# Scores and copy of head 0 in a differential-attention encoder: tile 1 in the second session, the copy further up

## The chip, the cores and the metric

The kernel runs on one core of one Trainium2 chip. The metric is the device time of one execution in microseconds (us), the median of several. All durations below are microseconds unless marked ns.

## The reference

Two layers over a sequence of 512 rows with 1024 features. Each layer has a mixer of three branches (a gated causal convolution with layer norm and silu, a differential attention, a spatial gate), a cross attention to 256 memory rows, and a convolutional feed-forward part. What matters here is the attention branch, and that the convolution's norm runs beside it:

```python
def one_block(args):                       # one of 4 blocks of 128 queries
    ...
    logits = jnp.einsum('bqhmd,bkhmd->bhmqk', q_blk, k).astype(f32) * scale + bias[None, :, None]
    logits = jnp.where(visible, logits, NEG_INF)
    p = jax.nn.softmax(logits, axis=-1)
    attn = p[:, :, 0] - lam * p[:, :, 1]   # two maps per head
    return jnp.einsum('bhqk,bkhe->bqhe', attn.astype(v.dtype), v)

merged = (gates[:, :, 0] * (ya @ w_br[0]) + gates[:, :, 1] * (yb @ w_br[1])
          + gates[:, :, 2] * (yc @ w_br[2]))
```

There are 4 heads with 2 maps (m = 0, 1) of 64 features each. A query block qb sees the keys up to its own block, so its score tile is 128 x 128(qb+1).

## The kernel before, in words

Every product of the model is done in three terms: each operand is split into a rounded head and a tail (the rest), and TensorE adds head x head, head x tail and tail x head. The weights come in units of 128 x 2048, numbered 0 to NU-1 in each layer (`plan`). A unit goes through four hands: SyncE loads it into `raw` (L571), ScalarE rounds it to `w_hd`, VectorE (or GpSimd) makes `w_tl` as the difference, and TensorE uses it (`product`, L1699, L1700 for the head terms, L1715 for the tail term). There are two buffers of each, so unit g+2 is loaded when the tail of unit g is made. Most products write two PSUM banks (a pair) and may start only when the pair's last product has been read (label `ev...`).

Each engine's program is one list, written out by hand in order of the units k: nothing is scheduled, and each engine does its list strictly in that order. All ScalarE work goes through the helper at L724. Engines wait for each other by counters: `line.done` marks an instruction with labels, `line.need`, `line.at` wait for them.

The attention is spread over the units 13 to 26 behind their products (`ATT`). Head h has these jobs:

- A (unit 13+3h) and B (unit 14+3h): TensorE makes the score tiles of both maps (`attention`). Map 0 uses rows 0 to 63 of the array and map 1 rows 64 to 127, so two neighbouring tiles of different maps run side by side. `TILES_OF` says which tiles, in pairs, `SC_AT` into which bank and column. For heads 0, 1 and 3 each tile is made of three terms, head 2 has one fp32 product. A takes query blocks 0, 1 and 2, B takes block 3. Tile (0, 1) and tile (1, 1) lie in bank 6 both, so the second waits for the first (`A_first`).
- VectorE reads each tile (`scores`, L1147), adds the bias and takes the row's maximum; ScalarE takes exponentials; VectorE combines the two maps (`combine`, L1159 to L1165) and turns the result in blocks of 32 x 32 (L1168). SyncE sends it to DRAM and back in four pieces (L546, L549, `turn`), and ScalarE copies them in order (label `att`, 128 x 1280).
- D (unit 16+3h): TensorE multiplies the probabilities with the values (L1808) into bank 7 (`misc`). It waits for that copy.

`IN_ORDER_AT` places the copies: head h's behind the two tanh of the gate in unit 16+3h. Beside head 0 runs the norm of the convolution: its sums are turned by TensorE in unit 15 (`conv_sums`, L1587, into bank 7), VectorE scales four tiles (L1437), ScalarE makes of each tile an affine form and its tanh (in unit 15, behind `CLN + 2`), and VectorE multiplies them (L1442). Behind these stand, in unit 16, VectorE's reads of the gate product (L1319), ScalarE's two tanh on them, and the copy of head 0.

Of the kernel before, what the change touches and what calls it, by code (L numbers as in the profile page):

```python
# [37 lines left out]
HEADS = 4  # L38
# [195 lines left out]
ATT0 = 13  # L234
# [4 lines left out]
for _h in range(HEADS):  # L239
    ATT.setdefault(ATT0 + 3 * _h + 3, []).insert(0, ("D", _h))  # L240
    if _h >= MOVED:
# [6 lines left out]

SO = [0, 128, 384, 768]
SC_AT = {(0, 0): (4, 384), (0, 1): (6, 0), (0, 2): (4, 0), (0, 3): (4, 0),  # L250
         (1, 0): (5, 384), (1, 1): (6, 256), (1, 2): (5, 0), (1, 3): (5, 0)}

TILES_OF = {"A": ((0, 1), (1, 2), (0, 2), (1, 0), (0, 0), (1, 1)), "B": ((0, 3), (1, 3))}
QK_HEADS = {11: (0, 1), 20: (3,)}
QK_TAILS = {21: 3}
QK_AT = {0: (4, 6), 1: (5, 7), 3: (2, 3)}
YA_ROUNDED = CLN + 5
IN_ORDER_AT = {ATT0 + 3 * _h + 3: _h for _h in range(HEADS)}
TURN_AT = {ATT0 + 3 * _h + 6: _h for _h in range(HEADS)}
OUT_AT = {ATT0 + 3 * _h + 8: _h for _h in range(MOVED)}  # L260

# [101 lines left out]
def build(nc, x_t, mem_t, units, pvec, bs, lam, w_st, rel_bias, onehot, ident_in, out, counts):  # L363
    ctx = ExitStack()
    with ctx:
# [26 lines left out]
        moved = s_sb[:, 0, :].rearrange("p (a t j) -> p t a j", a=4, j=32)  # L392
# [321 lines left out]
        def _(act):  # L714
# [100 lines left out]
            def cross_heads(h):  # L815
                op(y_hd[:, h, :], ps[:, X_OUT[h], :], labels=(f"yx_head{h}",), needs=(f"xpv{h}",))

            def heads_of_outputs(k):
                for h in YB_SPLIT.get(k, ()):
                    if h == 2:  # L820
                        act.wait_ge(tensor_done, line.at("B3"))
                    if h < MOVED:
                        act.wait_ge(o_in, 64 * (l * MOVED + h + 1))
                        op(in_order(y_hd[:, h, :]), turned_rows(q_sb[:, h, :]), ACT.Identity, (f"yb_head{h}",),
                           scale=col(l, "sub_g"))
                    else:
                        op(y_hd[:, h, :], q_sb[:, h, :], labels=(f"yb_head{h}",), needs=(f"ot{h}",))

            for l in range(DEPTH):
                line.begin(l)  # L830
                for k in range(NU):
                    for e, kind, arg in () if last_units(l, k) else UNIT_KINDS[k]:
# [14 lines left out]
                        elif kind == "u":  # L847
                            view = u_sb[:, 2 * arg:2 * arg + 2, :]
                            op(view, view, ACT.Gelu_apprx_tanh, (f"gelu_u{arg}",), (f"ev{e}",))
                        elif kind in ("w", "v"):  # L850
                            dst, f = (vn, ACT.Gelu_apprx_tanh) if kind == "w" else (v_sb, ACT.Copy)
                            for t in range(TB if arg else 0):
                                op(dst[:, t, :], ps[:, WIDE_BANK[kind] + t, :], f, (f"ev{e - 1 + t // 2}",),
                                   ("n0_rs", f"{kind}_tokens{t}"), scale=rs0[:, t:t + 1])
                            if arg:
                                next_head(k)
                        elif kind == "sv":
                            if arg == 0:
                                squares("c", lambda t: cg[:, C_OUT[t], PAD:], range(KB), lambda t: (f"c_cent{t}",))
                            for g in (2 * arg, 2 * arg + 1):  # L860
                                op(y_hd[:, g, :], tmp[:, g, :], labels=(f"yc_head{g}",), needs=(f"yc_src{g}",))
                        elif kind in ("gg", "g2"):
                            pos, j = arg
                            if kind == "g2":
                                j -= 1
                            if k == LAST_TURN:
                                heads_of_outputs(k)
                            for i in range(2):
                                view = tmp[:, gate_at(pos, j) + i, :]
                                op(view, view, ACT.Tanh, (f"th_g{pos}_{j + i}",), (f"raw_g{pos}_{j + i}",),  # L870
                                   scale=0.5, bias=col(l, "gate_b", BRANCH_OF[pos] * KD + j + i))
                            if k in IN_ORDER_AT:
                                h = IN_ORDER_AT[k]
                                act.wait_ge(att_in, 64 * (l * HEADS + h + 1))
                                op(att_t.rearrange("p t (a j) -> p t a j", a=4), moved, labels=(f"att{h}",))
                        elif kind == "xk":
                            op(kx_hd[:, 2 * arg:2 * arg + 2, :], ps[:, b:b + 2, 0:MEM], labels=(f"kx_head{arg}",))
                        elif kind == "xq" and arg == 0:
                            next_head(k)
                            query_heads(0, e)  # L880
                        elif kind == "up":
                            f0 = 4 * (arg % 2)
                            if arg == FIRST_UPS - 1:
                                next_head(k)
                            for i in range(2):
                                c = arg + NF * i
                                op(ft[:, f0 + i, :], tmp[:, 2 * (arg % 2) + i, :], ACT.Identity, (f"lin{arg}_{i}",),
                                   (f"up_src{arg}_{i}",) + ((f"act_tail{arg - 2}",) if arg >= 2 else ()),
                                   scale=col(l, "ffn_w", 3 * c + 2), bias=col(l, "ffn_b", c))
                            next_head(k + 1 if arg == FIRST_UPS - 1 else k)  # L890
                            op(ft[:, f0 + 2, :], ft[:, f0, :], ACT.Tanh, (f"th_f{arg}",), (f"conv_f{arg}_0",), scale=0.5)
                            op(ring_hd[:, arg % 8, :], ft[:, f0 + 2, :], labels=(f"act_head{arg}",),
                               needs=(f"act_src{arg}",), scale=0.5)
# [18 lines left out]
                    if k == CLN + 2:  # L912
                        for i in range(KB):
# [2 lines left out]
                               (f"c_norm{i}", "cs") + ((f"ya_src{i - 2}",) if i >= 2 else ()),  # L916
                               scale=col(l, "cln_g", i), bias=col(l, "cln_b", i))
                            op(th, z, ACT.Tanh, (f"th_c{i}",), (), scale=0.5)
                    for h in QK_HEADS.get(k, ()):
                        if h == 3:  # L920
                            act.wait_ge(tensor_done, line.at(f"e{ENTRY_OF['bb', (0, 6)]}"))
# [83 lines left out]
        def _(dve):  # L1005
# [132 lines left out]
            def scores(job, h):  # L1138
# [3 lines left out]
                for n, (m, qb) in enumerate(TILES_OF[job]):  # L1142
# [6 lines left out]
                        in1=bias_t[:, h % 2, S - w:S], scale=1.0, scalar=-3.0e38, op0=ALU.add, op1=ALU.max,  # L1149
                        accum_out=mx[:, 4 * m + qb:4 * m + qb + 1]), f"sc_free{job}_{h}", needs=(f"{job}{h}",) + free,  # L1150
                       plain=True, independent=min(n, 1))
                part = slice(0, 3) if job == "A" else slice(3, 4)
                op(lambda: dve.tensor_scalar(mneg.rearrange("p (m q) -> p m q", q=4)[:, :, part],
                                             mx.rearrange("p (m q) -> p m q", q=4)[:, :, part], -1.0, None, ALU.mult),
                   f"neg{job}_{h}")
# [414 lines left out]
        def _(pe):  # L1570
# [206 lines left out]
            def attention(job, h):  # L1777
                if job in "AB":
# [10 lines left out]
                        parts = ((q_sb[:, h], k_sb[:, h]),)  # L1789
                    for n in range(0, len(TILES_OF[job]), 2):  # L1790
                        pair = TILES_OF[job][n:n + 2]
                        if (1, 1) in pair:
                            pe.wait_ge(tensor_done, line.at(f"A_first{h}"))
                        for p, (q, key) in enumerate(parts):
                            for m, qb in pair:
                                bank, c0 = SC_AT[m, qb]
                                rows = slice(64 * m, 64 * m + 64)
                                i = pe.matmul(ps[:, bank, c0:c0 + P * (qb + 1)], q[rows, P * qb:P * qb + P],  # L1798
                                              key[rows, 0:P * (qb + 1)], start=p == 0, stop=p == len(parts) - 1)
                                if (m, qb) == (0, 1) and p == len(parts) - 1:  # L1800
                                    line.done(i, f"A_first{h}")
                    line.done(i, f"{job}{h}")
                elif job == "D":
                    pe.wait_ge(scalar_done, line.at(f"att{h}"))
# [63 lines left out]
                spread("n0", 4, rs0)  # L1868

            def conv_sums():  # L1870
                turned_sums("c", "c_cent3")

            for l in range(DEPTH):
                line.begin(l)
# [249 lines left out]
```

## Time and profile before

| | us |
|---|---|
| median of 3 runs | 1760.96 (1760.45 to 1761.63) |
| the profiled execution | 1761.88 |
| its span | 1760.1 |
| TensorE busy | 1741.1 (99%) |
| VectorE busy | 1287.1 (73%) |
| ScalarE busy | 745.7 (42%) |
| GpSimd busy | 491.3 (28%) |
| mean granted TensorE clock | 0.995 |

The profile is one execution; its times count from the span's start. An engine is busy while it works on an instruction; a matmul's end is modelled, so the start of the next one is the surer mark. In square brackets behind a row stands the idle time ahead of it and what ended it. PEld is TensorE's loading of weights, which lies beside the matmuls.

### The profile page before, as it was taken

How to read it: one execution, taken by the hardware profiler on the slowest of the kernel's cores; microseconds unless marked ns; L12 is line 12 of the kernel's file. 1: busy time of each engine (PE TensorE's matmuls, PEld its weight loads, DVE VectorE, ACT ScalarE, POOL GpSimd, SP SyncE). 2: the span in 40 equal slices, each digit the busy share in tenths (PEclk: the TensorE clock that was granted, in tenths of full speed). 3: DMA queues.
4: the chain of work that ended last, by engine and by line, in shares of the span. 5: the costliest groups of instructions: out<-in, count | busy, mean ns of one | idle time of the engine just before them, and what ended most of it. 6: DMA issues, size and time to landing. Idle time of an engine off the chain costs nothing. (4 is left out here: it accounts for less than half of the span.)

```text
span 1760.1 us, 21739 instructions
## 1 busy us (share of the span) xinstructions
PE 1741.1 (99%) x8127; PEld 1447.8 (82%) x8127; DVE 1287.1 (73%) x1696; ACT 745.7 (42%) x951; POOL 491.3 (28%) x204
## 2 busy tenths in 40 slices
PE   9999899999999999999999998999999999999998
PEld 7888788888888888888888887888888888888888
DVE  7998768664678776577779786775746797685585
ACT  4234555443564443343432345553445544343343
POOL 4453000103034244444133620010030332444440
PEclk9999999999999999999999999999999999999999
DMA  6532244422322332232232323444222223322321
GB/s 216 191 120 72 102 165 137 172 96 96 120 75 94 120 109 85 98 117 82 110 144 72 144 72 120 168 140 148 96 96 96 96 96 120 118 74 96 120 74 71
DMA packets 40777, 199.60 MB, mean 113 GB/s; under 512 B 4828, under 2 KB 14300, under 8 KB 20320
## 3 DMA queue, kind: packets, MB, share of 16 engines
q1 hardware_dynamic: 38460, 186.35, 30.0%
q0 software_dynamic: 1648, 11.54, 1.7%
q8 instruction: 64, 1.05, 0.2%
q10 hardware_dynamic: 564, 0.33, 0.1%
q14 instruction: 41, 0.34, 0.1%
HBM read 186.06 MB, written 14.49 MB: 114 GB/s over the span
## 5 line engine op out<-in xcount | busy, mean ns | idle before, releaser
L1699 PE MATMUL ps<-x_hd,w_hd 128*128 128x512 f32 x1568 | 612.3, 390 | 0.1
L1700 PE MATMUL ps<-x_tl,w_hd 128*128 128x512 f32 x1568 | 610.4, 389 | 0.0
L606 POOL TENSOR_TENSOR w_tl<-raw,w_hd 128x2048 fp32r<-128x2048 f32 x79 | 366.0, 4632 | 534.5 <-ACT w_hd L724 392.6
L724 ACT ACTIVATE w_hd<-raw 128x2048 fp32r<-128x2048 f32 (+2 forms) x159 | 298.1, 1875 | 321.7 <-PE ps L1700 231.9
L1715 PE MATMUL ps<-x_hd,w_tl 128*128 128x512 f32 x1568 | 373.4, 389 | 0.0
L1699 PEld LDWEIGHTS ps<-x_hd,w_hd 128*128 128x128 f32 x1568 | 294.3, 188 | 62.6 <-issue 0.7
L1715 PEld LDWEIGHTS ps<-x_hd,w_tl 128*128 128x128 f32 x1568 | 294.1, 188 | 61.0
L1700 PEld LDWEIGHTS ps<-x_tl,w_hd 128*128 128x128 f32 x1568 | 294.4, 188 | 60.5
L1699 PE MATMUL ps<-ring_hd,w_hd 128*128 128x512 f32 (+1 forms) x640 | 241.1, 381 | 0.0
L1700 PE MATMUL ps<-ring_tl,w_hd 128*128 128x512 f32 (+1 forms) x640 | 239.8, 379 | 0.0
L1402 DVE SCALAR_TENSOR_TENSOR merged<-merged 128x512 f32<-128x512 f32 x44 | 183.4, 4167 | 20.7 <-ACT merged L724 20.2
L1019 DVE TENSOR_TENSOR w_tl<-raw,w_hd 128x2048 fp32r<-128x2048 f32 x71 | 163.4, 2302 | 38.7 <-ACT w_hd L724 27.5
L1265 DVE TENSOR_TENSOR resid<-resid,ps 128x512 f32<-128x512 f32 x120 | 77.1, 684 | 115.0 <-PE ps L1715 111.8
L1181 DVE SCALAR_TENSOR_TENSOR ps<-cg,pv_all,ps 128x512 f32<-128x512 f32 x232 | 154.5, 747 | 0.0
L1715 PE MATMUL ps<-ring_hd,w_tl 128*128 128x512 f32 (+1 forms) x640 | 151.5, 379 | 0.0
L1699 PEld LDWEIGHTS ps<-ring_hd,w_hd 128*128 128x128 f32 x640 | 120.4, 188 | 26.7 <-issue 3.0
L1700 PEld LDWEIGHTS ps<-ring_tl,w_hd 128*128 128x128 f32 x640 | 120.4, 188 | 22.2
L1715 PEld LDWEIGHTS ps<-ring_hd,w_tl 128*128 128x128 f32 x640 | 115.9, 188 | 22.4
L724 ACT ACTIVATE ring_hd<-merged 128x512 fp32r<-128x512 f32 x44 | 27.8, 633 | 225.2 <-DVE merged L1404 225.2
L724 ACT ACTIVATE merged<-tmp,pv_all 128x512 f32<-128x512 f32 x88 | 71.9, 817 | 117.3 <-DVE tmp L1382 113.2
L1393 DVE SCALAR_TENSOR_TENSOR merged<-tmp,pv_all,merged 128x510 f32<-128x510 f32 (+1 forms) x176 | 120.2, 744 | 0.9 <-ACT merged L724 0.9
L1382 DVE TENSOR_TENSOR tmp<-ps,sq 128x512 f32<-128x512 f32 x88 | 56.7, 686 | 82.4 <-PE ps L1715 81.7
(229 smaller groups left out, 1654.0 us busy)
## 6 DMA issues: line engine op xcount, KB each, us to landing
raw<-units SPq DMA_DIRECT2D x154, 1024.0 KB, 4.8
att_dram<-s_sb SPq DMA_DIRECT2D x8, 640.0 KB, 2.9
s_sb<-att_dram SPq DMA_DIRECT2D x32, 160.0 KB, 3.4
bias_t<-bias_tiles POOLq DMA_DIRECT2D x8, 256.0 KB, 5.5
cg<-mem_t POOLq DMA_DIRECT2D x2, 1024.0 KB, 7.2
resid<-x_t POOLq DMA_DIRECT2D x1, 2048.0 KB, 8.1
resid_dram<-resid POOLq DMA_DIRECT2D x1, 2048.0 KB, 7.4
resid<-resid_dram POOLq DMA_DIRECT2D x1, 2048.0 KB, 8.2
```

Source lines behind the costliest of these rows:

```text
L606: line.done(pool.tensor_tensor(w_tl[:, k % 2, :], raw[:, k % 2, :], w_hd[:, k % 2, :].bitcast(F32), ALU.subtract), of_unit("tail", g))
L724: line.done(act.activation(out, in_, func, **kw), *labels)
L1019: op(lambda: dve.tensor_tensor(w_tl[:, slot, :], raw[:, slot, :], w_hd[:, slot, :].bitcast(F32), ALU.subtract), of_unit("tail", g), needs= ...
L1181: op(lambda: dve.scalar_tensor_tensor(dst, src, w, acc, ALU.mult, ALU.add), independent=1)
L1265: op(lambda: dve.tensor_tensor(dst, dst, ps[:, banks(e) + i, :], ALU.add), f"{tag}_{j + i}", f"ev{e}", needs=(f"e{e}",), independent=i)
L1382: op(lambda: dve.tensor_tensor(src, ps[:, b + i, :], r_all, ALU.mult), f"up_src{arg}_{i}", f"ev{e}", needs=(f"e{e}",), independent=i)
L1393: op(lambda: dve.scalar_tensor_tensor(dst[:, sh:S], src[:, 0:S - sh], col(l, "ffn_w", 3 * c + 2 - sh), dst[:, sh:S], ALU.mult, ALU.add), f ...
L1402: op(lambda: dve.scalar_tensor_tensor(th, th, 1.0, ft[:, f0, :], ALU.add, ALU.mult), needs=(f"th_f{arg}",))
L1699: pe.matmul(dst, w_hd[:, slot, w], hd[:, src, :], start=kc == 0, stop=False)
L1700: i = pe.matmul(dst, w_hd[:, slot, w], tl[:, src, :], start=False, stop=False)
L1715: i = pe.matmul(dst, w_tl[:, slot, w], hd[:, src, :], start=False, stop=kc == nk - 1)
```

## The change

Two things are moved, for both layers. Tile (0, 1) and tile (1, 1) of every head go from A to B; (0, 1) stays in bank 6 and (1, 1) goes to bank 7, the bank of the sums and of D. With that the wait `A_first` goes, A and B have equal tiles in every pair, the slices of the negated maxima follow, and the conv sums wait for the last reading of B0 as well. And the copy of head 0 goes from unit 16 to unit 15, behind the affine form and the tanh of the second conv tile; the copies of heads 1 to 3 stay.

```diff
 SC_AT = {(0, 0): (4, 384), (0, 1): (6, 0), (0, 2): (4, 0), (0, 3): (4, 0),
-         (1, 0): (5, 384), (1, 1): (6, 256), (1, 2): (5, 0), (1, 3): (5, 0)}
-TILES_OF = {"A": ((0, 1), (1, 2), (0, 2), (1, 0), (0, 0), (1, 1)), "B": ((0, 3), (1, 3))}
+         (1, 0): (5, 384), (1, 1): (7, 0), (1, 2): (5, 0), (1, 3): (5, 0)}
+TILES_OF = {"A": ((0, 2), (1, 2), (0, 0), (1, 0)), "B": ((0, 3), (1, 3), (0, 1), (1, 1))}
...
-IN_ORDER_AT = {ATT0 + 3 * _h + 3: _h for _h in range(HEADS)}
+IN_ORDER_AT = {ATT0 + 3 * _h + 3: _h for _h in range(1, HEADS)}
...
+            def probabilities_in_order(h):
+                act.wait_ge(att_in, 64 * (l * HEADS + h + 1))
+                op(att_t.rearrange("p t (a j) -> p t a j", a=4), moved, labels=(f"att{h}",))
...
                             op(th, z, ACT.Tanh, (f"th_c{i}",), (), scale=0.5)
+                            if i == 1:
+                                probabilities_in_order(0)
...
-                part = slice(0, 3) if job == "A" else slice(3, 4)
+                part = slice(0, 4, 2) if job == "A" else slice(1, 4, 2)
...
-                        if (1, 1) in pair:
-                            pe.wait_ge(tensor_done, line.at(f"A_first{h}"))
...
-                                if (m, qb) == (0, 1) and p == len(parts) - 1:
-                                    line.done(i, f"A_first{h}")
...
-                turned_sums("c", "c_cent3")
+                turned_sums("c", "c_cent3", "sc_freeB_0")
```

**ScalarE, units 14 to 16 of layer 0.** `sq<-cg` and `cg<-sq` are a conv tile's affine form and tanh, `tmp<-tmp` the tanh of unit 16's gate, 128x1280 the copy of head 0, `w_hd<-raw` the heads of units 17 and 18. Before:

```order
L724 ACTIVATE w_hd<-raw 128x2048 [waits scalar_done,weights_in1,tensor_done]
L724 ACTIVATE sq<-cg,pv_all 128x512 [waits scalar_done,tensor_done,vector_done]
L724 ACTIVATE cg<-sq 128x512 [waits scalar_done]
L724 ACTIVATE sq<-cg,pv_all 128x512 [waits scalar_done,tensor_done,vector_done]
L724 ACTIVATE cg<-sq 128x512 [waits scalar_done]
L724 ACTIVATE sq<-cg,pv_all 128x512 [waits scalar_done,tensor_done,vector_done]
L724 ACTIVATE cg<-sq 128x512 [waits scalar_done]
L724 ACTIVATE sq<-cg,pv_all 128x512 [waits scalar_done,tensor_done,vector_done]
L724 ACTIVATE cg<-sq 128x512 [waits scalar_done]
L724 ACTIVATE tmp<-tmp,pv_all 128x512 [waits scalar_done,vector_done] x2
L724 ACTIVATE s_sb<-s_sb 128x1280 [waits scalar_done,att_in]
L724 ACTIVATE w_hd<-raw 128x2048 [waits scalar_done,weights_in0,tensor_done]
```

Now:

```order
L724 ACTIVATE w_hd<-raw 128x2048 [waits scalar_done,weights_in1,tensor_done]
L724 ACTIVATE sq<-cg,pv_all 128x512 [waits scalar_done,tensor_done,vector_done]
L724 ACTIVATE cg<-sq 128x512 [waits scalar_done]
L724 ACTIVATE sq<-cg,pv_all 128x512 [waits scalar_done,tensor_done,vector_done]
L724 ACTIVATE cg<-sq 128x512 [waits scalar_done]
L724 ACTIVATE s_sb<-s_sb 128x1280 [waits scalar_done,att_in]
L724 ACTIVATE sq<-cg,pv_all 128x512 [waits scalar_done,tensor_done,vector_done]
L724 ACTIVATE cg<-sq 128x512 [waits scalar_done]
L724 ACTIVATE sq<-cg,pv_all 128x512 [waits scalar_done,tensor_done,vector_done]
L724 ACTIVATE cg<-sq 128x512 [waits scalar_done]
L724 ACTIVATE tmp<-tmp,pv_all 128x512 [waits scalar_done,vector_done] x2
L724 ACTIVATE w_hd<-raw 128x2048 [waits scalar_done,weights_in0,tensor_done]
```

The copy has moved ahead of the third and fourth conv tile and of the gate's tanh; these and the head of unit 18 stand behind it and its wait for `att_in`.

**TensorE, the scores of head 0 in layer 0** (`ring_hd`, `ring_tl` are the split queries and keys; lines behind 816 stand 4 further down in the kernel after). The second and third pair of A, before:

```order
L1798 MATMUL ps<-ring_hd 128x384
L1798 MATMUL ps<-ring_hd 128x128
L1798 MATMUL ps<-ring_tl,ring_hd 128x384
L1798 MATMUL ps<-ring_tl,ring_hd 128x128
L1798 MATMUL ps<-ring_hd,ring_tl 128x384
L1798 MATMUL ps<-ring_hd,ring_tl 128x128
L1798 MATMUL ps<-ring_hd 128x128 [waits tensor_done]
L1798 MATMUL ps<-ring_hd 128x256
L1798 MATMUL ps<-ring_tl,ring_hd 128x128
L1798 MATMUL ps<-ring_tl,ring_hd 128x256
L1798 MATMUL ps<-ring_hd,ring_tl 128x128
L1798 MATMUL ps<-ring_hd,ring_tl 128x256
```

A now, and the first instruction of unit 14:

```order
L1800 MATMUL ps<-ring_hd 128x384 [waits vector_done]
L1800 MATMUL ps<-ring_hd 128x384
L1800 MATMUL ps<-ring_tl,ring_hd 128x384 x2
L1800 MATMUL ps<-ring_hd,ring_tl 128x384 x2
L1800 MATMUL ps<-ring_hd 128x128 x2
L1800 MATMUL ps<-ring_tl,ring_hd 128x128 x2
L1800 MATMUL ps<-ring_hd,ring_tl 128x128 x2
L1703 MATMUL ps<-x_hd,w_hd 128x512 [waits vector_done,scalar_done]
```

B of head 0 now, whose first four rows were all of it before:

```order
L1800 MATMUL ps<-ring_hd 128x512 [waits vector_done]
L1800 MATMUL ps<-ring_hd 128x512
L1800 MATMUL ps<-ring_tl,ring_hd 128x512 x2
L1800 MATMUL ps<-ring_hd,ring_tl 128x512 x2
L1800 MATMUL ps<-ring_hd 128x256 x2
L1800 MATMUL ps<-ring_tl,ring_hd 128x256 x2
L1800 MATMUL ps<-ring_hd,ring_tl 128x256 x2
```

The 256-wide tiles are gone from A, with the wait inside it, and stand at the end of B.

## Rows read from the trace of the kernel before

**Rows 1.** Waits of TensorE: engine line <- what released it: us, times, longest.
```profile
PE ps L1808 <- ACT s_sb L724: 11.1, 2, 5.7
```

**Rows 2.** Order of time, TensorE, units 16 and 17: start us, us, engine line operation.
```profile
200.06 1.98 PE L1715 MATMUL ps<-ring_hd,w_tl 128*128 128x512 f32 x8
...
207.78 4.64 PE L1808 MATMUL ps<-v_sb,s_sb 128*128 128x128 f32 x20 [5.75 <-ACT s_sb L724]
...
214.36 0.50 PE L1699 MATMUL ps<-x_hd,w_hd 128*128 128x512 f32 x1
...
1077.93 4.63 PE L1808 MATMUL ps<-v_sb,s_sb 128*128 128x128 f32 x20 [5.33 <-ACT s_sb L724]
...
1084.64 0.50 PE L1699 MATMUL ps<-x_hd,w_hd 128*128 128x512 f32 x1
```

**Rows 3.** Windows, layer 0: us; PE, PEld, DVE, ACT, POOL busy (x); granted clock.
```profile
206.00:208.00 2.00, 0.22 (x1) 0.22 (x2) 0.96 (x2) 1.79 (x3) 0.00 (x0) 0.72 0.00 0
...
210.00:212.00 2.00, 2.00 (x12) 2.00 (x10) 0.00 (x0) 0.00 (x0) 0.00 (x0) 0.50 0.00 0
```

**Rows 4.** Order of time, TensorE: head 2 D, head 3 A, product; head 3 B, product.
```profile
286.24 2.39 PE L1808 MATMUL ps<-v_sb,s_sb 128*128 128x128 f32 x20
...
288.56 0.44 PE L1798 MATMUL ps<-ring_hd 64*128 64x256 f32 x2
...
289.97 0.50 PE L1699 MATMUL ps<-x_hd,w_hd 128*128 128x512 f32 x1
...
301.07 0.50 PE L1798 MATMUL ps<-ring_hd 64*128 64x512 f32 x2
...
301.97 0.50 PE L1699 MATMUL ps<-ring_hd,w_hd 128*128 128x512 f32 x1
```

**Rows 5.** Order of time, ScalarE, units 14 to 16 of layer 0.
```profile
184.85 0.72 ACT L724 ACTIVATE s_sb<-s_sb,mneg 128x512 f32<-128x512 f32 x1 [0.74 <-DVE mneg L1153]
...
199.46 0.63 ACT L724 ACTIVATE cg<-sq 128x512 f32<-128x512 f32 x1
...
206.46 1.27 ACT L724 ACTIVATE s_sb<-s_sb 128x1280 f32<-128x1280 f32 x1
```

**Rows 6.** The four pieces (L549) of head 0: issues, first and last start, landing; both layers.
```profile
L549 SPq DMA_DIRECT2D s_sb<-att_dram x4: 340/432/433, 195.3 to 196.6; - x4
...
DMA to landing us min/median/max: 2.8/3.3/3.7
...
L549 SPq DMA_DIRECT2D s_sb<-att_dram x4: 326/432/434, 1065.5 to 1066.8; - x4
...
DMA to landing us min/median/max: 2.8/3.5/4.6
```

**Rows 7.** Order of time, VectorE, units 13 to 16 of layer 0.
```profile
172.46 0.42 DVE L1147 CUSTOM_DVE_ANT_0 s_sb<-ps,bias_t 128x256 f32<-128x256 f32 x1 [0.29 <-DVE tmp L1338]
...
172.81 0.08 DVE L1147 DVE_READ_ACCUMULATOR2_ANT mx<- 128x1 f32 x1
...
183.30 0.69 DVE L1147 CUSTOM_DVE_ANT_0 s_sb<-ps,bias_t 128x512 f32<-128x512 f32 x1 [0.17 <-issue]
...
184.64 0.17 DVE L1153 TENSOR_SCALAR mneg<-mx 128x2 f32<-128x2 f32 x1
...
188.35 0.20 DVE L1159 RECIPROCAL rc<-sm 128x8 f32<-128x8 f32 x1
...
204.11 1.29 DVE L1319 TENSOR_TENSOR tmp<-ps,r 128x512 f32<-128x512 f32 x2
...
212.46 1.13 DVE L1194 TENSOR_SCALAR tmp<-ps,rc 128x128 f32<-128x128 f32 x4 [5.37 <-PE ps L1808]
```

**Rows 8.** Order of time, units 13 and 15: VectorE's bank read, then TensorE.
```profile
165.30 1.62 DVE L1333 SCALAR_TENSOR_TENSOR tmp<-ps,pv_all,wsbs 128x512 f32<-128x512 f32 x2
...
167.06 0.47 PE L1699 MATMUL ps<-x_hd,w_hd 128*128 128x512 f32 x1
...
182.78 0.60 PE L1587 MATMUL ps<-ident,ssum 128*128 128x128 f32 x4
```

More of the change, by code:

```diff
@@ L872, in _ @@
                             if k in IN_ORDER_AT:
-                                h = IN_ORDER_AT[k]
-                                act.wait_ge(att_in, 64 * (l * HEADS + h + 1))
-                                op(att_t.rearrange("p t (a j) -> p t a j", a=4), moved, labels=(f"att{h}",))
+                                probabilities_in_order(IN_ORDER_AT[k])
                         elif kind == "xk":
```

## The prediction

> **What bounds the kernel now.** I read the table of the page first: TensorE is busy 99% of 1760.1 us, so only time in which it stands still, runs at the low clock or streams more columns than it must can be won. The view of waits, for TensorE, has one entry over 2 us: twice, 11.1 us in all, it waits for ScalarE before the matmuls of L1808 [rows 1]. These are the value products of head 0 (job D, unit 16), once in each layer. The order of time shows the place [rows 2]: unit 16's last product starts at 200.06 and lasts 1.98, and D0 starts at 207.78, after 5.75 idle; in layer 1 the idle is 5.33 before 1077.93.
>
> The wait costs more than itself. The windows [rows 3] show the granted clock at a mean 0.72 in 206 to 208 and 0.50 in 210 to 212: TensorE went from 2.4 to 1.2 GHz while it stood idle, near 206.9. So D0 and the scores of head 1 behind it (A1) take 6.58 (207.78 to 214.36) and 6.71 (1077.93 to 1084.64) [rows 2], where D of head 2 and A of head 3 take 3.73 at full clock (286.24 to 289.97) [rows 4].
>
> What D0 waits for is the copy that puts the turned probabilities in order (206.46 to 207.73) [rows 5]. ScalarE does it behind the two tanh of unit 16's gate, and these behind the whole conv chain. Its data were there long before: the four pieces were issued at 195.3 to 196.6 and took at most 3.7 to land, so by 200.3; in layer 1, 1066.8 plus at most 4.6, so by 1071.4 [rows 6].
>
> **Part 1: the copy moves up.** It now stands behind the second tanh of the conv chain, which ends at 200.09 [rows 5], in layer 1 at 1070.24 (that layer runs the same pattern 870.15 later: 1077.93 against 207.78). So it starts at about 200.3 and 1071.4 (the landing decides), takes 1.27, and is done at 201.6 and 1072.7, before TensorE comes to D0. The wait is gone. What is queued behind the copy on ScalarE now comes later: the third and fourth conv tiles. In layer 0 they slip 1.4 (copy and step), in layer 1, where ScalarE also stands 1.1 for the last piece, 2.5. VectorE's last conv step and then its two gate reads (204.11 on, 1.29 for both) [rows 7] slip by as much: the second read ends at 206.9 instead of 205.4, and at 1078.0 instead of 1075.55. TensorE needs that read: it frees the banks of unit 17's product, which stands behind A1.
>
> **Part 2: tile 1 in the second session.** In a session both maps run side by side on 64 rows each. The session A of before streams 768 columns per map and term (128, 256, 384) and B 512; now A has 512 and B 768. The two swap. From [rows 4]: A took 1.41 (288.56 to 289.97) and B 0.90 (301.07 to 301.97). So A should cost 0.9 to 1.05 now (two of its tiles are only 128 wide; I take 1.0) and B 1.22 (0.90 plus 3 times 256 columns at 2.4 GHz, 0.32) to 1.41. Over a head that is -0.2 to +0.15: nothing. But A0's part is not won at all: the product behind it starts at 167.06, and VectorE's read of its banks ends at 166.92 [rows 8], so TensorE waits there instead.
>
> VectorE drops two 256-wide score steps in A and adds them in B, 0.35 each (172.46 to 172.81) [rows 7]. It works without a pause here, so B0's scoring starts 0.7 to 1.0 earlier, at about 182.4, and ends after about 1.25 (183.30 to 184.64, less the step to the negation) plus 0.70, at about 184.3. In layer 1 it is the same within 0.2. ScalarE's exponentials of B0 start at 184.85 now [rows 5], so at about 184.5; four of at most 0.9 each (0.72 and the read of the sum behind it) end by 188.1, and VectorE takes up the sums at 188.35 [rows 7]. So the turned probabilities leave at their old time.
>
> **Part 3: the added wait.** Bank 7 now holds scores of B0, so the conv sums in unit 15 also wait for B0's scoring. They start at 182.78 now [rows 8], and would stand at 183.1 after the longer B0. They get in at about 184.3, so TensorE idles 1.1 to 1.2 in each layer. I bound this by 0 (VectorE comes earlier) and 1.9 (nothing of A's saving reaches B0). All behind it is 1.45 later: unit 16 ends near 203.5 (202.05 plus 1.45) and near 1074.05.
>
> **The sum**, at the start of unit 17's product. Layer 0: TensorE is at D0 at 203.5, D0 takes 2.32 (286.24 to 288.56) [rows 4], A1 1.0, so 206.8; the gate read ends at 206.9; start at 206.95 against 214.36, -7.4. Layer 1: 1074.05 plus 2.32 plus 1.0 is 1077.4, but the read ends at 1078.0; start at 1078.1 against 1084.64, -6.5. Of each about 4 is idle, 2.8 the clock; 0.1 to 0.75 goes back to the new wait for the gate read. In the rest of a layer B1, A2, B2, A3 and B3 add and save in turn: +0.3, -0.4, +0.4, -0.4, +0.3, so +0.2, and +0.5 for both layers. -7.4 - 6.5 + 0.5 is -13.4.
>
> Does it stay? Behind unit 17, VectorE stood idle 5.37 before it could read D0 (212.46) [rows 7]; this reserve is used up, but by my count of its list (gate merge to 208.4, reading of D0, scoring of A1, tail weights) it is done with unit 18's tails near 213.6, and TensorE needs them near 223, behind unit 17's 48 products, B1 and unit 18's head terms. Nothing later waits for a fixed time: loads follow the tails, the tails follow TensorE. I cost the later units at zero for that reason; without this cover each us VectorE is late is one us per layer.
>
> The profiled execution took 1761.9, of which 1760.1 are the span; so 1748.5 for it. The median of the runs is 0.9 lower: **1747.6 us**.
>
> **Rivals.**
>
> *The wait moves further (14%).* The gate read, or the last piece, comes later than I read it, and unit 17's product stands still. For it: in layer 1 one piece already took 4.6, and VectorE, ScalarE and TensorE meet here within 0.1 to 0.7. Against it: in layer 0 no piece took over 3.7. Each us is paid once per layer; 2 us in each give 1751.6.
>
> *The clock falls once more (4%).* If the idle of 1.1 at unit 15, or one at unit 17, brings the low level as now, about 2.8 comes back per layer, what D0 and A1 lose to it now (6.58 against 3.73) [rows 2, 4]: 1753.2. Against it: at full idleness the clock held from 202.0 to 206.9.
>
> *Slower: the clock stays low through units 15 to 17 (3%).* The new wait is followed by short blocks (four transposes, the spread, D0), and if TensorE stayed at 1.2 GHz from 184.3 to 206.9, 22.5 us of work would take twice as long: +22.5 and -6.7 per layer, 1792.6. It decides from the point where the low stretch holds more than 6.7 us of full-speed work. Against it: the only low stretch of now costs 2.8 in all, although D0 and A1 in it are short blocks. The Trainium skill (TensorE: Matmul & The Clock Gate, "A second HAM failure mode: psum-queue depth-cycling") describes such a kernel: short idles between groups of matmuls make the clock swing between its two levels. By that rule this change, which puts three short idles where one long one was, would be the 1792.6; this trace does not show it, since its one fall follows the one long idle.
>
> *It does not do what it says (2%).* If the pieces landed 5 us later than their rows, D0 would wait as before and the time stay at about 1760.
>
> **Numbers.** My forecast has 77%. Measured against no change, about 0.2% (3.5 us) can be told apart. Faster by more: forecast and the first two rivals, 0.95. Within: 0.02. Slower: 0.03. The low end of the range has the added wait at 0, no wait for the gate read and A and B at their low values (-2.3, -0.9, -1.3): 1743.1. The high end takes in the first two rivals: 1753.5.
>
> **What would show it.** In the profile of the changed kernel: no wait of L1808's group for ScalarE; a granted clock of 1.00 from 200 to 216; the copy between the second and third conv tile; about 1.1 idle before the conv sums, ended by VectorE's scoring; the value products of head 0 at 2.3 instead of 4.6; unit 17's product at 207.0 and, with layer 0's gain, near 1071. Wrong would be a new pause in front of unit 17 of over 2 us, a low clock in units 15 to 17, or a gain at unit 17 that is gone by unit 22.

## The result, and the profile after

The changed kernel takes 1748.12 us, the median of 6 runs (1747.71 to 1749.45); the kernel before takes 1761.05 (6 runs, 1759.82 to 1761.63). The ratio is 0.9929, 95% interval 0.9916 to 0.9941. 12.9 us are gone; 13.4 were predicted. The profiled execution took 1749.45 with a span of 1747.6, and its mean granted clock is 0.999 where it was 0.995.

The view of waits, for TensorE, lists what is left (the line numbers stand 4 higher than before):

```profile
PE ps L1591 <- DVE mx L1151: 2.2, 2, 1.3
...
PE ps L1703 <- ACT tmp L724: 1.1, 1, 1.1
PE ps L1703 <- DVE tmp L1337: 0.9, 2, 0.5
```

The value products (L1808) are not in it any more: of their 11.1 us [rows 1] nothing is left. In their place stand the conv sums (L1591), which wait for VectorE's scoring of B0, and once the product of unit 17 (L1703). The third line is 0.45 in each layer before the product behind A0 (167.75 in layer 0), where the prediction had said that TensorE would wait for VectorE's read instead of winning A's shorter time. TensorE in order of time, layer 0 and then layer 1: conv sums, last product of unit 16, D0, A1, product of unit 17:

```profile
185.28 0.66 PE L1591 MATMUL ps<-ident,ssum 128*128 128x128 f32 x4 [1.30 <-DVE mx L1151]
...
202.57 1.98 PE L1719 MATMUL ps<-ring_hd,w_tl 128*128 128x512 f32 x8
204.39 2.39 PE L1808 MATMUL ps<-v_sb,s_sb 128*128 128x128 f32 x20
206.71 0.44 PE L1800 MATMUL ps<-ring_hd 64*128 64x384 f32 x2
...
207.83 0.47 PE L1703 MATMUL ps<-x_hd,w_hd 128*128 128x512 f32 x1
...
1048.42 0.66 PE L1591 MATMUL ps<-ident,ssum 128*128 128x128 f32 x4 [0.92 <-DVE mx L1151]
...
1067.53 2.39 PE L1808 MATMUL ps<-v_sb,s_sb 128*128 128x128 f32 x20
1069.85 0.44 PE L1800 MATMUL ps<-ring_hd 64*128 64x384 f32 x2
...
1071.99 0.47 PE L1703 MATMUL ps<-x_hd,w_hd 128*128 128x512 f32 x1 [1.07 <-ACT tmp L724]
```

These rows answer to [rows 2]: D0 takes 2.32 (204.39 to 206.71) and A1 1.12, where the two took 6.58. In the windows the granted clock stays at 1.00, so 2.4 GHz, where [rows 3] had 0.72 and 0.50; the last three windows are 8 us long and begin at the conv sums of each layer and at unit 17 of layer 1:

```profile
206.00:208.00 2.00, 1.95 (x21) 1.72 (x20) 1.70 (x4) 0.79 (x2) 0.00 (x0) 1.00 0.00 0
208.00:210.00 2.00, 2.00 (x10) 1.61 (x10) 1.76 (x4) 1.89 (x2) 0.00 (x0) 1.00 0.00 0
...
184.00:192.00 8.00, 6.72 (x32) 5.66 (x33) 7.47 (x17) 3.44 (x10) 1.02 (x1) 1.00 0.57 227
1048.00:1056.00 8.00, 7.58 (x36) 6.36 (x37) 7.47 (x15) 4.27 (x9) 1.02 (x1) 1.00 0.47 181
1071.00:1079.00 8.00, 7.01 (x31) 5.83 (x32) 7.11 (x18) 6.88 (x17) 0.00 (x0) 1.00 0.00 0
```

ScalarE in order of time, the copy in both layers, and VectorE's two reads of unit 16's gate product behind it:

```profile
201.09 1.27 ACT L724 ACTIVATE s_sb<-s_sb 128x1280 f32<-128x1280 f32 x1 [0.40 <-DMA s_sb<-att_dram]
...
1065.27 1.27 ACT L724 ACTIVATE s_sb<-s_sb 128x1280 f32<-128x1280 f32 x1 [1.42 <-DMA s_sb<-att_dram]
```

```profile
206.39 1.29 DVE L1323 TENSOR_TENSOR tmp<-ps,r 128x512 f32<-128x512 f32 x2
...
1070.55 1.29 DVE L1323 TENSOR_TENSOR tmp<-ps,r 128x512 f32<-128x512 f32 x2
```

The copy now waits for its data (0.40 and 1.42), where before the data waited for the copy. In layer 1 the second gate read ends at 1071.84 and unit 17's product starts at 1071.99. The bracket there names ScalarE's tanh, but the start lies 0.15 behind the end of the read; in the first experiment below, where the bracket names VectorE, it lies 0.14 behind (1070.38 plus 1.29, against 1071.81). It is the read that TensorE waits for. The same holds in layer 0: the read ends at 207.68 and unit 17's product starts at 207.83, 0.15 behind. No bracket stands there, because the modelled ends of A1's matmuls cover it; but where the read is early (the copy behind the third tile, below) A1 takes 1.00 from start to start, not 1.12, so about 0.12 of it is this wait.

**Where the time came from.** The two profiled executions, part by part, at the starts of TensorE's rows (the marks 161.40, 1031.94 and 1196.28 of before are 162.09, 1025.60 and 1183.88 now):

| stretch | before | after | difference |
|---|---|---|---|
| start to the first mark, ahead of the change | 161.40 | 162.09 | +0.69 |
| to unit 17 of layer 0 | 52.96 | 45.74 | -7.22 |
| to the mark in layer 1 | 817.58 | 817.77 | +0.19 |
| to unit 17 of layer 1 | 52.70 | 46.39 | -6.31 |
| to the mark behind the attention | 111.64 | 111.89 | +0.25 |
| to the end | 563.82 | 563.72 | -0.10 |
| sum | 1760.1 | 1747.6 | -12.50 |

The first line is no effect of the change: the first 162 us are the same program, and the profiled executions of the kernels below lie between 161.28 and 162.03 there. Nothing was given back later.

The rows also say what the two gains are made of. Layer 0: the idle before D0 was 5.75 and 1.30 of new idle stands before the conv sums, so 4.45; D0 and A1 take 3.44 instead of 6.58, so 3.14, of which 0.29 is A1's (1.12 instead of 1.41) and the rest the clock; B0 costs 0.36 more. That is 7.23. Layer 1: 5.33 less 0.92 and 1.07 is 3.34; D0 and A1 without the idle behind them take 3.39 instead of 6.71, so 3.32; less 0.36 that is 6.30.

The scores of head 3 answer to [rows 4]. The starts of A3, the product behind it, B3 and the product behind that:

```profile
282.31 0.44 PE L1800 MATMUL ps<-ring_hd 64*128 64x384 f32 x2
...
283.30 0.50 PE L1703 MATMUL ps<-x_hd,w_hd 128*128 128x512 f32 x1
...
294.41 0.50 PE L1800 MATMUL ps<-ring_hd 64*128 64x512 f32 x2
...
295.67 0.50 PE L1703 MATMUL ps<-ring_hd,w_hd 128*128 128x512 f32 x1
```

A takes 0.99 instead of 1.41, B 1.26 instead of 0.90.

### The profile page after: what moved, and what is told of

It is laid out like the page before. It is cut to its first block and busy times, and to the rows that moved or that the text cites. A ratio compares the mean times of both kernels' runs of the same rounds, so it can differ in the third digit from the quotient of the medians.

```text
span 1747.6 us, 21739 instructions
## 1 busy us (share of the span) xinstructions
PE 1735.7 (99%) x8127; PEld 1442.4 (83%) x8127; DVE 1286.9 (74%) x1696; ACT 745.7 (43%) x951; POOL 490.7 (28%) x204
## 5 line engine op out<-in xcount | busy, mean ns | idle before, releaser
L1703 PE MATMUL ps<-x_hd,w_hd 128*128 128x512 f32 x1568 | 612.2, 390 | 2.0 <-ACT tmp L724 1.1
L1703 PEld LDWEIGHTS ps<-x_hd,w_hd 128*128 128x128 f32 x1568 | 294.3, 188 | 64.2 <-issue 2.8
L1703 PE MATMUL ps<-ring_hd,w_hd 128*128 128x512 f32 (+1 forms) x640 | 241.2, 381 | 0.0
L1703 PEld LDWEIGHTS ps<-ring_hd,w_hd 128*128 128x128 f32 x640 | 120.3, 188 | 24.5 <-issue 0.7
```

The source lines that it names most:

```text
L1703: pe.matmul(dst, w_hd[:, slot, w], hd[:, src, :], start=kc == 0, stop=False)
```

## Experiments

My theory: the whole gain is the copy's (idle and clock), and the tiles bring nothing. The rivals: the tiles carry a part of it; the new wait at the conv sums costs its full length; the clock falls in other places too. Diffs are against the changed kernel except where said.

### The copy alone

Bank, tiles and `A_first` are those of the kernel before; against that kernel:

```diff
-IN_ORDER_AT = {ATT0 + 3 * _h + 3: _h for _h in range(HEADS)}
+IN_ORDER_AT = {ATT0 + 3 * _h + 3: _h for _h in range(1, HEADS)}
...
                             op(th, z, ACT.Tanh, (f"th_c{i}",), (), scale=0.5)
+                            if i == 1:
+                                probabilities_in_order(0)
```

> Only the copy of head 0 is moved; the tiles stay as before. Theory (the whole gain is the copy): D0 starts when TensorE comes to it, 1.45 us earlier than in the change since the added wait is absent; but unit 17's product is held by VectorE's gate read (206.9 and 1078.0 on before's times), so it starts where the change's does; 13.4 to 14.4 us below before, 1746.6 to 1747.6. Rival (the moved tiles bring part of the gain): at least 2 us above the change, 1750 or more.

Measured: 1748.93 (4 runs, 1747.75 to 1749.76), ratio to before 0.9931 (0.9915 to 0.9948). The changed kernel's ratio is 0.9929, so the two can't be told apart. The forecast of 1746.6 to 1747.6 was 1.3 too low at its near end, and the rival's 1750 or more did not come either. From the marks of the table to unit 17 this kernel takes 46.15 and 46.17, the changed one 45.74 and 46.39: the same sum within 0.2. In its view of waits the conv sums are missing, and the wait before unit 17 is longer:

```profile
PE ps L1703 <- DVE tmp L1323: 3.0, 2, 1.5
```

In order of time it stands in both layers:

```profile
208.18 0.47 PE L1703 MATMUL ps<-x_hd,w_hd 128*128 128x512 f32 x1 [1.49 <-DVE tmp L1323]
...
1071.81 0.47 PE L1703 MATMUL ps<-x_hd,w_hd 128*128 128x512 f32 x1 [1.49 <-DVE tmp L1323]
```

So TensorE gets to unit 17 earlier and waits there for the gate read. In the changed kernel 2.2 us stand before the conv sums and 1.1 before unit 17: the tiles move most of this wait further up, and the time stays.

### The tiles alone

```diff
-IN_ORDER_AT = {ATT0 + 3 * _h + 3: _h for _h in range(1, HEADS)}
+IN_ORDER_AT = {ATT0 + 3 * _h + 3: _h for _h in range(HEADS)}
...
-                            if i == 1:
-                                probabilities_in_order(0)
```

> Only the tiles are moved; the copy stays where it was. Theory: D0 still waits for the copy, which VectorE and ScalarE reach at the same time as before, so D0 starts at 207.8 again, after 4.3 us of idle instead of 5.75, because the added wait stands ahead of it; +0.5 us for the rest, 1761.5, if the clock falls as before. If 4.3 us of idle no longer bring the low clock, D0 and A1 give back 2.8 us per layer and it is 1755.5. Rival (the tiles bring part of the gain by themselves): 1757 to 1759 with the clock falling as before.

Measured: 1760.14 (10 runs, 1757.63 to 1761.44), ratio 0.9994 (0.9984 to 1.0003): no difference that can be told from noise, where 1761.5 was forecast, and not the rival's 1757 to 1759. The idle before D0 is 1.9 and 1.5 shorter than before [rows 2], since the later conv sums take it up (4.3 instead of 5.75 was forecast, it is 3.85). The clock falls all the same. In layer 0 the low stretch is shorter, from 207.8 to 211.2, and in layer 1 as long as before, 6.8 us, although the two idles are alike; the ten executions have mean clocks of 0.995 to 0.998, so this differs between executions too. D0 in both layers, the windows of layer 0, and one of 8 us in layer 1:

```profile
207.62 4.13 PE L1806 MATMUL ps<-v_sb,s_sb 128*128 128x128 f32 x20 [3.85 <-ACT s_sb L724]
...
1076.45 4.64 PE L1806 MATMUL ps<-v_sb,s_sb 128*128 128x128 f32 x20 [3.84 <-ACT s_sb L724]
```

```profile
206.00:208.00 2.00, 0.38 (x2) 0.39 (x3) 0.79 (x2) 1.79 (x3) 0.00 (x0) 0.94 0.00 0
208.00:210.00 2.00, 2.00 (x11) 2.00 (x11) 0.00 (x0) 1.59 (x1) 0.00 (x0) 0.50 0.00 0
210.00:212.00 2.00, 2.00 (x15) 1.88 (x15) 0.22 (x1) 0.00 (x0) 0.00 (x0) 0.70 0.00 0
...
1074.00:1082.00 8.00, 5.55 (x30) 5.33 (x30) 2.31 (x7) 4.12 (x4) 0.00 (x0) 0.57 0.00 0
```

### The copy later: behind the third and the fourth tanh

```diff
-                            if i == 1:
+                            if i == 2:
```

> The change, with the copy behind the third conv tile's tanh instead of the second's. Theory: in layer 1 ScalarE no longer stands for the last piece (1.4 us in the change), the gate read comes 1.1 us earlier and TensorE's wait before unit 17 (1.07 us) goes; in layer 0 nothing moves: 1 us below the change. Rival (that wait is not the gate read's): same as the change within 0.3 us, with the wait still there.

Measured: 1748.09 (4 runs, 1747.85 to 1748.3), ratio 0.9927 (0.9913 to 0.9942), so no different from the change, where 1 us less was forecast. The trace does show the forecast: in layer 1 the copy finds its data landed, the wait before unit 17 is gone, and from the mark to unit 17 that layer takes 45.26 instead of 46.39. The changed kernel's profiled execution was the slowest of its six (1749.45, median 1748.12); perhaps the others had less of this wait, but no trace of them exists.

```profile
1065.43 1.27 ACT L724 ACTIVATE s_sb<-s_sb 128x1280 f32<-128x1280 f32 x1
```

With `i == 3`, behind the last tanh:

> The change, with the copy behind the fourth conv tile's tanh. Theory: ScalarE reaches the copy at 204.0 (layer 0) and 1067.1 (layer 1) on the change's times and ends it 0.9 to 1.0 us after TensorE stands at D0; the gate read is 1.4 and 2.8 us earlier, so nothing waits before unit 17. Layer 0 +0.9, layer 1 -0.2: 0.7 us above the change, with a wait of L1808 for ScalarE of 1.0 us in each layer. Rival (the place of the copy within the conv chain does not matter): the change's time and no wait of D0.

Measured: 1749.91 (4 runs, 1749.5 to 1750.62), ratio 0.9936 (0.9921 to 0.9952). Now D0 waits for the copy again, 0.77 in each layer where 1.0 was forecast, and nothing waits before unit 17. To unit 17 the two layers take 0.94 more and 0.09 less than in the changed kernel, as forecast (+0.9 and -0.2); the medians lie 1.8 apart, and the four runs (from 1749.5) all lie above the six of the change (up to 1749.45).

```profile
204.52 2.50 PE L1808 MATMUL ps<-v_sb,s_sb 128*128 128x128 f32 x20 [0.77 <-ACT s_sb L724]
...
1068.60 2.50 PE L1808 MATMUL ps<-v_sb,s_sb 128*128 128x128 f32 x20 [0.77 <-ACT s_sb L724]
```

The three places lie within 1.8 us of each other and all over 11 us below before. What matters most is that the copy leaves the place behind the gate's tanh; among the places ahead of it, the place decides only which waits of 1.5 or less are left.

### The conv sums wait longer, for the tail of unit 16

```diff
             def conv_sums():
+                pe.wait_ge(vector_done, line.at(of_unit("tail", l * NU + 16)))
                 turned_sums("c", "c_cent3", "sc_freeB_0")
```

> The change, with the conv sums waiting also for the tail weights of unit 16, which VectorE makes behind B0's scoring; TensorE then idles 3.7 us there instead of 1.3 (layer 0) and 3.4 instead of 0.9 (layer 1). Theory: each us is paid once, less the wait before unit 17 in layer 1 that it hides: +2.4 and +1.3, 3.7 us above the change, and the clock stays at 2.4 GHz. Rival (an idle of this length brings the low clock too): a granted clock of 0.5 somewhere in units 15 to 17 and 2 to 6 us more on top.

Measured: 1756.54 (9 runs, 1755.73 to 1757.66), ratio 0.9976 (0.9966 to 0.9985): 8.4 above the change. The theory that only the added idle counts fell, and its rival held. TensorE in order of time, both layers, and the windows of layer 0:

```profile
187.57 0.66 PE L1591 MATMUL ps<-ident,ssum 128*128 128x128 f32 x4 [3.91 <-DVE w_tl L1023]
...
1054.84 0.66 PE L1591 MATMUL ps<-ident,ssum 128*128 128x128 f32 x4 [3.55 <-DVE w_tl L1023]
```

```profile
186.00:188.00 2.00, 0.43 (x5) 0.43 (x5) 1.51 (x1) 1.79 (x5) 0.00 (x0) 1.00 0.00 0
188.00:190.00 2.00, 2.00 (x10) 1.58 (x8) 1.53 (x5) 0.23 (x2) 0.76 (x1) 0.72 0.72 184
190.00:192.00 2.00, 2.00 (x6) 1.58 (x5) 1.97 (x5) 0.00 (x0) 0.26 (x1) 0.50 0.83 348
```

The clock falls only when TensorE is already working again, at about 188.9, and is back at about 192.3. The added idles are 2.6 in each layer, of which layer 1 hides 1.1 in its old wait before unit 17, so 4.2; two low stretches of 3.4 at half speed cost 3.4. That is 7.6, and trace against trace the way from the mark to unit 17 is 4.15 and 3.13 longer, 7.3. The traces leave nothing over; the medians lie 8.4 apart because the changed kernel's profiled execution was its slowest.

### Bank 7 read first

VectorE reads the tiles (0, 1) and (1, 1) of every B first, and the conv sums wait for these two alone (label `sc_seven_0` on head 0's read of bank 7, the second of them).

```diff
-                for n, (m, qb) in enumerate(TILES_OF[job]):
+                tiles = TILES_OF[job] if job == "A" else TILES_OF[job][2:] + TILES_OF[job][:2]
+                for n, (m, qb) in enumerate(tiles):
...
-                turned_sums("c", "c_cent3", "sc_freeB_0")
+                turned_sums("c", "c_cent3", "sc_seven_0")
```

> The change, but VectorE reads B0's tile in bank 7 ahead of the 512-wide tiles and the conv sums wait for that tile alone; nothing else moves. Theory: the wait of 1.3 and 0.9 us before the conv sums goes, TensorE comes to unit 17 that much earlier and waits there for the gate read, which stays where it is: the change's time within 0.4 us, with 1.2 and 2.0 us of idle before unit 17. Rival (the added wait costs its length): 2.2 us below the change.

Measured: 1749.32 (4 runs, 1749.03 to 1751.17), ratio 0.9932 (0.9914 to 0.995). The wait at the conv sums is gone and the time is no better: it has moved before unit 17, and in layer 1 to D0 as well, which waits 0.30 for the copy. TensorE in order of time, and the windows behind the second of these rows:

```profile
207.56 0.47 PE L1705 MATMUL ps<-x_hd,w_hd 128*128 128x512 f32 x1 [1.06 <-DVE tmp L1325]
...
1072.09 0.47 PE L1705 MATMUL ps<-x_hd,w_hd 128*128 128x512 f32 x1 [1.90 <-ACT tmp L724]
```

```profile
1072.00:1074.00 2.00, 1.91 (x6) 1.62 (x7) 1.63 (x3) 1.79 (x3) 0.00 (x0) 0.72 0.00 0
1074.00:1076.00 2.00, 2.00 (x6) 1.52 (x6) 1.72 (x7) 1.74 (x5) 0.00 (x0) 0.50 0.00 0
```

I had not expected the second of these rows to bring this: after 1.90 idle, with D0's 0.30 shortly before it, the clock went to 1.2 GHz. From 1072.86 to 1076.24 TensorE starts 8 matmuls, 0.42 apart; 0.23 apart they would take 1.8 instead of 3.4, so 1.6 is lost. The forecast (the change's time within 0.4) missed by that much in this execution. The profiled run took 1751.17, the three others 1749.03 to 1749.55, which fits a fall in the one and none in the others, at a mean clock of 0.998 against 0.999. Even these three lie 0.9 to 1.4 above the changed kernel's median.

### Idles of 2.4 and 3.3

To see from which idle on the clock falls, the conv sums wait for the first exponential of B0 on ScalarE, and in a second kernel for the second one (`expB_0_1_3`).

```diff
+                                op(view, view, ACT.Exp, (f"exp{job}_{h}", f"exp{job}_{h}_{m}_{qb}"), (f"neg{job}_{h}",),
...
             def conv_sums():
+                pe.wait_ge(scalar_done, line.at("expB_0_0_3"))
```

> The changed kernel, but the conv sums in unit 15 also wait for the first exponential of B0 on ScalarE. By the rows of the changed kernel that ends at 186.1 to 186.2 and TensorE starts at about 186.4 instead of 185.28: the idle grows from 1.30 to 2.4, in layer 1 from 0.92 to 2.0. Layer 1 stood 1.07 before unit 17 anyway, so it hides its share. Theory that only the idles of 3.5 and more bring the low clock: granted clock 1.00 from 184 to 194, time +1.1 for layer 0 and 0 to 0.2 for layer 1, so about 1749.3. Rival, that an idle of about 2 does it too, as the profiled run of the kernel with bank 7 read first hints (1.90 idle, then 0.50): the clock is 0.5 in 188 to 192, and each fall costs about 2.1 more (what the longer wait cost over its idles), so 1751.4 with one fall, 1753.5 with two.

> As the one before, but the wait is for the second exponential made (query block 3 of map 1), about 0.9 later: idle 3.3 in layer 0 and 2.9 in layer 1. Theory that only idles of 3.5 and more bring the low clock: clock 1.00 throughout, time +2.0 and +0.9, so about 1751.1. Rival, that it falls here too: +4.2 more, 1755.3, with windows of 0.50 in both layers.

The first: 1751.34 (4 runs), ratio 0.9944 (0.9927 to 0.996). Its profiled run took 1749.91 and shows the idles as meant and no fall. The two rows, and the window of 8 us about each:

```profile
185.83 0.66 PE L1591 MATMUL ps<-ident,ssum 128*128 128x128 f32 x4 [2.35 <-ACT s_sb L724]
...
1049.94 0.66 PE L1591 MATMUL ps<-ident,ssum 128*128 128x128 f32 x4 [1.98 <-ACT s_sb L724]
```

```profile
184.00:192.00 8.00, 6.17 (x29) 5.18 (x30) 7.48 (x17) 2.83 (x8) 1.02 (x1) 1.00 0.53 199
1048.00:1056.00 8.00, 6.06 (x29) 5.09 (x30) 7.47 (x17) 2.84 (x8) 1.02 (x1) 1.00 0.57 208
```

The three others took 1751.31 to 1751.47 at a mean clock of 0.998 against 0.999. So the profiled execution is near the theory's 1749.3 and the three others at the rival's 1751.4 with one fall: the same kernel holds the clock in one execution and, as far as mean clock and time tell, loses it once in the others. In which layer, no trace shows.

The second: 1755.09 (5 runs, 1754.39 to 1755.27), ratio 0.9964 (0.9951 to 0.9977), mean clock 0.997 in all five. The profiled one shows both outcomes, a fall after 3.25 in layer 0, and none after 2.89 in layer 1:

```profile
186.70 1.12 PE L1591 MATMUL ps<-ident,ssum 128*128 128x128 f32 x4 [3.25 <-ACT s_sb L724]
...
1054.44 0.66 PE L1591 MATMUL ps<-ident,ssum 128*128 128x128 f32 x4 [2.89 <-ACT s_sb L724]
```

```profile
184.00:186.00 2.00, 0.00 (x0) 0.00 (x0) 1.83 (x6) 0.98 (x3) 0.00 (x0) 0.90 0.63 266
186.00:188.00 2.00, 1.30 (x5) 1.25 (x6) 1.47 (x2) 1.81 (x6) 0.00 (x0) 0.50 0.00 0
...
190.00:192.00 2.00, 2.00 (x6) 1.52 (x6) 1.97 (x4) 0.00 (x0) 0.00 (x0) 0.50 0.75 307
...
1052.00:1060.00 8.00, 5.56 (x27) 4.65 (x28) 7.47 (x15) 2.83 (x8) 1.02 (x1) 1.00 0.46 185
```

By the medians it costs 7.0 over the change, near the rival's 1755.3; but of the rival's two falls the profiled execution has one, in a stretch twice as long. Trace against trace the way from the mark to unit 17 is 4.55 longer in layer 0 and 0.87 in layer 1, 5.4. The idles explain 2.9 (3.25 less 1.30 in layer 0; 2.89 less 0.92 in layer 1, of which 1.07 is hidden in the old wait before unit 17), the low stretch, in which TensorE works from 186.70 to about 192.4, another 2.8: 5.7, so nothing is left over in the traces. The rest of the 7.0 lies between executions: the changed kernel's profiled one was its slowest, this kernel's its fastest.

### All three waits taken away

VectorE makes the weight tail of unit 17 (2.3 us) ahead of the conv tiles, and later stands idle for ScalarE's tanh. Here the tail comes behind the second conv step (`ya_src1`), in that pause, and all four tiles, the tanh and the gate read come earlier. The copy stands behind the fourth tanh, where its data have landed or nearly so:

```diff
-                            if i == 1:
+                            if i == 3:
...
-                    if k in TAIL_MID:
+                    if k in TAIL_MID and k != CLN + 2:
...
+                            if i == 1:
+                                tail_of_unit(l * NU + k + 2)
```

> The copy behind the fourth conv tile as in the run before, and VectorE makes unit 17's tail weights behind the second conv tile's last step instead of ahead of the norm, so the conv chain runs 2.4 us earlier. Theory: the copy ends at 203.0, ahead of TensorE (204.4), the gate read near 205; no wait at D0 and none before unit 17; layer 0 the same as the change, layer 1 1.1 us earlier: 1.1 us below the change. Rival (tail weights made later hold unit 17 or the loads behind them): slower than the change, with a wait of L1715's products for VectorE.

Measured: 1748.0 (4 runs, 1747.85 to 1748.22), ratio 0.9925 (0.991 to 0.9941). No wait is left at D0 or unit 17, only the one at the conv sums. As with the copy behind the third tile, the forecast 1.1 shows in the trace (45.66 and 45.28 to unit 17, against 45.74 and 46.39) and not in the medians. With bank 7 read first added to it:

> The norm first, the copy behind the fourth conv tile, and VectorE reading bank 7's tile first. Theory: now that neither the gate read nor the copy holds TensorE, the 1.3 and 0.9 us before the conv sums are won as well: 1.1 + 2.1 = 3.2 us below the change, 1744.9. Rival (the added wait never cost anything): same as the run without the changed order.

Measured: **1745.51** (4 runs, 1745.44 to 1745.73), ratio 0.9911 (0.9896 to 0.9927). All of its waits of TensorE of 0.5 us or more:

```profile
PE ps L1611 <- POOL ones L627: 1.1, 1, 1.1
PE ps L1707 <- DVE tmp L1339: 0.9, 2, 0.5
PE ps L1956 <- POOL rs L623: 0.5, 1, 0.5
```

The forecast was 3.2 below the change, 2.6 came. Neither of the two edits alone gained anything that the runs can tell apart (1748.0 and 1749.32 against 1748.12). Together they bring 2.6, and 2.5 over the first of them alone, whose conv sums still wait 2.2. That 2.2 is worth something only once the gate read behind it is no longer late. Whether bank 7 read first on top of the copy behind the third tile would do as much was not run; there the gate read ends only 0.37 and 0.34 before unit 17's product starts, so it should run into it again.

## Why the prediction was right, and where it was off

The forecast was 1747.6 in a range of 1743.1 to 1753.5; 1748.12 came out, by the mechanism it named. Point by point:

- **The wait at D0 goes, and the clock stays up.** Right. The copy alone gives the whole gain, the tiles alone none that can be told from noise; -7.22 and -6.31 up to unit 17 stand against -7.4 and -6.5, and idle and clock share it as forecast (about 4 and 2.8 in layer 0; 3.3 and about 3 in layer 1).
- **The copy's time.** The landing decides, as forecast. In layer 1 the last piece took 4.9, where 4.6 was the largest [rows 6]; the copy waited 1.42, where I had 1.1. With bank 7 read first the last piece took 5.2 there.
- **The added wait.** Forecast 1.1 to 1.2 in each layer, measured 1.30 and 0.92. B0's scoring came 0.77 earlier against its surroundings (183.22, less the 0.69 of the start, against 183.30 [rows 7]), at the near end of my 0.7 to 1.0. The exponentials and the turned probabilities left at their old time, as forecast: the pieces were issued from 195.9 on, less 0.69 that is 195.2, against 195.3 [rows 6].
- **The gate read before unit 17.** The sum had 0.15 in layer 0 and 0.7 in layer 1; measured 0.12 (inside the 1.12 from A1's start to unit 17's) and 1.07. In layer 1 TensorE came earlier (its conv sums waited only 0.92) and the piece later.
- **A and B.** Forecast 1.0 and 1.22, measured 0.99 and 1.26. Over the rest of both layers +0.5 was forecast and +0.34 came (0.19, 0.25 and -0.10).
- **VectorE's reserve.** It is done with unit 18's tails at 215.0 (212.75 plus 2.29), less the start's 0.69 at 214.4, where I had counted 213.6; TensorE did not wait for them.
- **Rival "the wait moves further".** It has its germ in the 1.07 of layer 1; at 2 us per layer, as that rival had it, it did not come.
- **Rival "the clock falls once more".** It did not happen in the changed kernel, but my reason against it was wrong. I took it as evidence that the clock had held through 4.9 us of full idleness (202.0 to 206.9). The kernel with bank 7 first shows 1.2 GHz after 1.90 of idleness, and the one with 3.25 shows it from about 185.6, when TensorE had stood for 2.1. An idle that is survived once is no bound. With what is known now I would have given this rival more than 4%. No execution of the changed kernel shows a fall by its mean clock (0.999 or 1.0 in all six); whether an idle of 1.3 can bring one stays open.
- **Rival "slower: the clock stays low".** The rule of the Trainium skill (TensorE: Matmul & The Clock Gate, "A second HAM failure mode: psum-queue depth-cycling") would have had the clock swing with the short idles. This case's trace does not agree: with idles of 1.30, 0.92 and 1.07 the granted clock is 1.00 around all three. The short idle of 1.90 that did bring a fall brought one of 3.4 us, not a clock that stays low.

That the tiles bring nothing was said of the streamed columns, and holds. What the prediction did not say is that the wait they add costs nothing either, and only because the gate read was late anyway.

## What to carry to other kernels

A wait of TensorE that is long enough to lower its clock is worth more than its length: 11.1 us of waiting gave 12.9 back although 2.2 and 1.1 of new waits came in. Look for short work of another engine that stands in its list behind something it does not need. When several engines meet within a microsecond or two, a single further edit may only move the wait, as the copy behind the fourth tile and bank 7 read first did here; look which engine releases each next start, and take those waits away together.

## What the hardware showed that I had not expected

Whether the clock falls after an idle is not a matter of the idle's length alone. In the profiled executions it never fell after 1.49 and less (sixteen idles of 0.77 to 1.49 around units 15 to 17), and always after 3.5 and more (3.91, 3.55, 3.85, 3.84, and 5.75 and 5.33 before). One execution of the copy alone, without a trace, had a mean clock of 0.998 and the longest time of its four (1749.76), so a fall after 1.49 is not ruled out. Between these it went both ways: a fall after 1.90 and after 3.25, none after 1.98, 2.35 and 2.89; and one kernel took 1749.91 in the execution whose trace shows no fall and 1751.3 to 1751.5 in three others. The low stretch also differs, and not by the idle's length: 3.4 us after 1.90, 3.55, 3.85 and 3.91, 6.8 after 3.25, 3.84, 5.33 and 5.75. So does its start, counted from the start of the idle: 2.1 us (idles 3.25 and 3.84), 2.7 (1.90), 4.0 (3.85), 4.9 (5.75), 5.2 (3.91). In four of the eight falls TensorE is already working again, so a look at the clock inside the idle alone misses them. The Trainium skill (TensorE: Matmul & The Clock Gate, "What's actually happening") calls the number of slow matmuls at a kernel's start variable from run to run; these traces agree (the same first eleven matmuls of the program take 4.32 us with bank 7 read first and 5.06 in the changed kernel), and show the like for idles in the middle of a kernel. So here an idle of about 2 to 3 us should be costed with a chance, not with a yes or no.
